# Half 0 of a two-layer block ahead of its expert stage: convolution, norm and output projection in another order, modulation sums in buffers of their own, weight slabs stored in rows of 8 KB

## What is computed

```python
mod = c_act @ w_mod + b_mod            # sh1, sc1, gt1, sh2, sc2, gt2
h = rmsnorm(x, ln_mix_g) * (1 + sc1) + sh1
q, kc, vc, ksl, vsl, kw, vw, gts, cb, cc, ch = split(h @ w_in)
o_attn = nsa_mixer(q, kc, vc, ksl, vsl, kw, vw, gts, ...)   # compressed, selected and window attention
o_conv = short_conv_mixer(ch, cb, cc, conv_w)               # cb * conv3(cc * ch)
mixed = concat(rmsnorm(o_attn, norm_attn_g), rmsnorm(o_conv, norm_conv_g))
x = x + gt1 * (mixed @ w_out)
h2 = rmsnorm(x, ln_ffn_g) * (1 + sc2) + sh2
x = x + gt2 * peer_ffn(h2, ...)
```

## Time and profile before

| | us |
|---|---|
| three runs | 1449.68, 1445.88, 1447.91 (median 1447.91) |
| profiled execution, its own time | 1451.15 |
| its span, first to last instruction | 1449.3 |

### The profile page before, as it was taken

The page is one execution under the profiler, slowest core; times in us unless marked ns, Lnnn a source line. Parts: engine busy times, 40 slices in busy tenths (PEclk is TensorE's granted clock), DMA queues, the critical chain, the costliest instruction groups (busy, mean ns, idle before and its releaser), DMA issues.

```text
span 1449.3 us, 15054 instructions
## 1 busy us (share of the span) xinstructions
PE 1160.8 (80%) x5592; PEld 674.0 (47%) x5592; DVE 745.7 (51%) x1811; ACT 487.0 (34%) x1283; POOL 370.6 (26%) x285
## 2 busy tenths in 40 slices
PE   6799885868867676666677766679988998999997
PEld 2588653422422231111122221134866887889883
DVE  5113468758769965465444445530455656652102
ACT  1022124443433433344333333321576543112201
POOL 0868202243434444433343433300000000000000
PEclk9998998999988999998998999989998999999999
DMA  9953605789999999999999999915422131114230
GB/s 365 304 218 146 246 1 201 308 326 416 412 414 420 410 412 397 421 421 407 423 386 404 396 401 422 421 65 176 174 68 107 59 117 60 60 59 160 73 116 29
DMA packets 92164, 377.58 MB, mean 261 GB/s; under 512 B 6355, under 2 KB 9596, under 8 KB 59260
## 3 DMA queue, kind: packets, MB, share of 16 engines
q0 software_dynamic: 36864, 268.45, 45.3%
q1 hardware_dynamic: 54560, 106.13, 20.4%
q10 hardware_dynamic: 668, 2.04, 0.4%
HBM read 375.54 MB, written 1.06 MB: 260 GB/s over the span
## 4 chain that ended last, share of the span: by engine, by line
PE 48%; DMA 24%; DVE 18%; ACT 7%; issue 2%; POOL 1%; SPq 1%; DVEq 0%; POOLq 0%; ACTq 0%
PE ps L87 48%; DMA AR<-in_puv,idx 20%; DVE AR L87 8%; DVE RT L87 3%; ACT L87 2%; DVE tok L87 2%; DMA mixT<-scr 1%; ACT av L87 1%; DMA W<-in_w_mod 1%; DVE acc L87 1%; DVE rowb L87 1%; DVE mixT L87 1%; ACT acc L87 1%; POOL AR L87 1%; ACT rowb L87 1%
## 5 line engine op out<-in xcount | busy, mean ns | idle before, releaser
L87 PE MATMUL ps<-AR,acc 128*64 128x512 f32 x960 | 371.2, 689 | 184.3 <-ACT acc L87 183.1
L87 POOL DMA_INDIRECT AR<-in_puv,idx x256 | 278.1, 1086 | 502.1 <-PE ps L87 394.0
L87 PE MATMUL ps<-hT,W 128*128 128x256 f32 (+2 forms) x1504 | 324.6, 374 | 2.6 <-ACT hT L87 2.5
L87 PEld LDWEIGHTS ps<-hT,W 128*128 128x128 f32 (+1 forms) x1504 | 270.4, 195 | 54.8 <-issue 15.9
L87 PEld LDWEIGHTS ps<-AR,acc 128*64 128x64 f32 x960 | 90.2, 149 | 439.3 <-ACT acc L87 356.8
L87 DVE CUSTOM_DVE_ANT_0 AR<-AR,mixT 128x1024 f32<-128x1024 f32 x128 | 156.7, 1227 | 157.0 <-DMA AR<-in_puv,idx 156.8
L87 DVE CUSTOM_DVE_ANT_0 AR<-AR,tok 128x1024 f32<-128x1024 f32 x128 | 153.1, 1219 | 66.3 <-DMA AR<-in_puv,idx 66.2
L87 ACT ACTIVATE av<-av 128x1 f32<-128x1 f32 x256 | 51.3, 200 | 311.5 <-DVE av L87 311.3
L87 ACT ACT_TABLE_LOAD x105 | 134.7, 1283 | 11.4 <-DVE tok L87 9.5
L87 PE MATMUL ps<-W,hT 128*128 128x512 f32 (+3 forms) x288 | 97.8, 497 | 0.8 <-ACT hT L87 0.8
L87 ACT ACTIVATE acc<-fold,av 128x64 f32<-128x64 f32 x240 | 83.5, 348 | 7.8
(11 more groups left out here) (230 smaller groups left out, 1087.5 us busy)
## 6 DMA issues: line engine op xcount, KB each, us to landing
W<-in_w_in SPq DMA_DIRECT2D x25, 2048.0 KB, 8.4
W<-in_w_mod SPq DMA_DIRECT2D x12, 2048.0 KB, 17.4
W<-in_w_out SPq DMA_DIRECT2D x2, 2048.0 KB, 10.3
W<-in_wq SPq DMA_DIRECT2D x2, 2048.0 KB, 10.2
AR<-in_puv,idx POOLq DMA_INDIRECT x256, 11.3
W<-in_wba SPq DMA_DIRECT2D x2, 2048.0 KB, 7.7
W<-in_wbb SPq DMA_DIRECT2D x2, 2048.0 KB, 8.6
W<-in_wo SPq DMA_DIRECT2D x2, 2048.0 KB, 7.7
```

The costliest lines, as they stand in the source:

```text
L87: ins = f(*args, **kw)
```

## The change

1. A slab is stored as 128 rows that each hold a partition's eight pieces of 512 floats one after another, and is loaded by two DMAs of 1 MB with rows of 8 KB (the slab of 280 and that of 16 columns have shorter ones in the tile).
2. The six modulation sums go to `RT`, `R_POST` and `R_LNF`, so they wait for nothing but their slab, and `flip_bias` moves behind the key and value projection. `conv_mix` and `attn_mix` no longer wait for the column sums.
3. `conv_step(0, 0)` and `conv_step(1, 0)` move between the two halves of the last convolution projection, with `weigh(3)` between them.
4. Behind the projections the attention's norm comes first, then the convolution's, then the two row sums (matmuls ahead of the mix, additions behind it); `attn_mm` waits part by part (`t_mk`). The column sums and `mod_affine` move behind `attn_mm(0, 1)`.
5. `scores(4)` no longer stands between the halves of the output projection: its matmuls stand behind `q_norm2`, its VectorE part behind `conv_mix(1)`. `weigh(4)`, `turn_p(4)`, `pv_(4)` and unit 5's scores become entries of `half1()`, which so has two entries more at its head.
6. The 29 pieces of routing ahead of the loop are gone; the loop advances 10 pieces a step for p < 3, 5 for p < 14, then 8.

```diff
         def load_w(i, after=()):
             if i < len(plan):
                 src, a, n = plan[i]
-                landed[i] = SP.dma(nc.sync.dma_start, wsem[i % NSLOT], W[:, i % NSLOT, :, 0:n],
-                                   src[:, a:a + n].rearrange("(k p) n -> p k n", p=P), after=after)
+                for k in (0, 4):
+                    landed[i] = SP.dma(nc.sync.dma_start, wsem[i % NSLOT], W[:, i % NSLOT, k:k + 4, 0:n],
+                                       src[:, 8 * a + k * n:8 * a + (k + 4) * n].rearrange("p (k n) -> p k n", k=4), after=after)
...
+        ms_buf = [RT[:, 512 * n:512 * n + 512] for n in range(3)] + [R_POST[:, 0:512], R_POST[:, 512:1024], R_LNF[:, 0:512]]
...
-        t_B = flip_bias()
...
         mod_next()
+        t_B = flip_bias()
...
                 run_step(2)
+                if (n, j2) == (2, 0):
+                    conv_step(0, 0)
+                    weigh(3)
+                    conv_step(1, 0)
...
-                       after=b.old + [t_w] + t_mix[a])
+                       after=b.old + [t_w, t_mk[a][k]])
...
-        for j in range(4):
-            conv_step(j, 0)
+        conv_step(2, 0)
+        conv_step(3, 0)
         turn_p(3)
         pv_(2)
-        b2 = ps.take()
-        for n in range(4):
-            t_mc.append(mod_cols_sum(b2, 4 * n, *t_ms[n]))
-        sh2, sc2, t_m2 = mod_affine(b2, t_mc[3], 24, V_LNF, 16)
+        pv_(3)
+        attn_root(0)
         norm_root(("c", 0), nrm[:, 0, :], cbT[:, :, 0:P], t_oc[0])
-        pv_(3)
+        rb = [mod_row_mm(*t_ms[4 + n]) for n in range(2)]
+        attn_mix(0)
         conv_mix(0)
         for n in range(2):
-            t_g1.append(mod_row_sum(2, n, *t_ms[4 + n]))
-        attn_root(0)
-        attn_mix(0)
+            t_g1.append(mod_row_add(2, n, *rb[n]))
         attn_mm(0, 0)
         for j in range(4):
             conv_step(j, 1)
         attn_add(0, 0)
-        scores(4)
         attn_mm(0, 1)
-        weigh(4)
+        b2 = ps.take()
+        for n in range(4):
+            t_mc.append(mod_cols_sum(b2, 4 * n, *t_ms[n]))
         attn_add(0, 1)
-        turn_p(4)
         norm_root(("c", 1), nrm[:, 1, :], cbT[:, :, P:2 * P], t_oc[1])
-        q_norm(0, [])
+        q_norm1(0)
+        sh2, sc2, t_m2 = mod_affine(b2, t_mc[3], 24, V_LNF, 16)
+        q_norm2(0, [])
+        scores_mm(4)
         q_project(0, 0)
         conv_mix(1)
...
+        scores_add(4)
         routes = [route(0, [])]
...
-        pv_(4)
         while (0, 0) not in t_idx or (0, 0) not in t_gw:
             advance(routes[0], 1)
-        scores_mm(5)
-        advance(routes[0], 29)
-        scores_add(5)
...
-            yield [lambda: weigh(5), lambda: scores_mm(6)]
+            yield [lambda: weigh(4), lambda: scores_mm(5)]
+            yield [lambda: scores_add(5), lambda: turn_p(4)]
+            yield [lambda: weigh(5), lambda: pv_(4), lambda: scores_mm(6)]
...
-            advance(routes[0], 4 if p < 12 else 8)
+            advance(routes[0], 10 if p < 3 else 5 if p < 14 else 8)
...
+    def slabs(w, cuts=None):
+        cuts = cuts or range(0, w.shape[1] + 1, 512)
+        return np.concatenate([w[:, lo:hi].reshape(8, P, hi - lo).transpose(1, 0, 2).reshape(P, -1)
+                               for lo, hi in itertools.pairwise(cuts)], axis=1)
```

More of the change, by code:

```diff
@@ L1 @@
+import itertools
 import math
@@ L235, in build @@
         R_LNF, R_POST, R_G1, R_G2 = (rowb[:, r, :] for r in range(4))
+        RT = sb("RT", [P, 6 * 256])
         t_neg = V(nc.vector.memset, tok2[32:33, 1, 0:8], NEG)
@@ L306, in mod_cols_sum, with mod_row_mm, mod_row_add @@
             return t2
-        def mod_row_sum(r, n, buf, t):
+        def mod_row_mm(buf, t):
             b = ps.take()
-            t = PE(mm, b.t[:, :], ones, buf, start=True, stop=True, after=b.old + [t, t_in])
+            return b, PE(mm, b.t[:, :], ones, buf, start=True, stop=True, after=b.old + [t, t_in])
+        def mod_row_add(r, n, b, t):
             o = rowb[:, r, n * 512:n * 512 + 512]
@@ L660, in build, with conv_step @@
                   lambda: (cmp_turn(0, 0), cmp_turn(0, 1)),
-                  lambda: (cmp_add(0, 0), cmp_add(0, 1), pv_(0), pv_(1), turn_p(2), scores(3), weigh(3)),
+                  lambda: (cmp_add(0, 0), cmp_add(0, 1), pv_(0), pv_(1), turn_p(2), scores(3)),
                   ]
+        def conv_step(j, a):
+            c0, c = a * P, slice(a * P, a * P + P)
+            wc = [PV[:, V_CW + r * 4 + j:V_CW + r * 4 + j + 1] for r in range(3)]
+            o = oc[:, j, c]
+            t = V(ts_, o, z[:, j, c0:c0 + P], wc[0], None, MUL, after=[t_cv[2, j // 2], t_zz])
+            t = V(stt, o, z[:, j, c0 + 1:c0 + 1 + P], wc[1], o, MUL, ADD, after=[t])
+            t = V(stt, o, z[:, j, c0 + 2:c0 + 2 + P], wc[2], o, MUL, ADD, after=[t])
+            t = V(tt_, o, o, cbT[:, j, c], MUL, after=[t, t_cv[0, j // 2]])
+            t_oc[a].append(V(tt_, cbT[:, j, c], o, o, MUL, after=[t]))
         oc = ccT
+        t_oc = [[], []]
         t_zz = G(nc.gpsimd.memset, z[:, :, 0:2], 0.0)
@@ L685, in build @@
                 run_step(2)
+                if (n, j2) == (2, 0):
+                    conv_step(0, 0)
+                    weigh(3)
+                    conv_step(1, 0)
         run_step(99)
-        t_oc = []
-        def conv_step(j, a):
-            c0, c = a * P, slice(a * P, a * P + P)
-            wc = [PV[:, V_CW + r * 4 + j:V_CW + r * 4 + j + 1] for r in range(3)]
-            o = oc[:, j, c]
-            t = V(ts_, o, z[:, j, c0:c0 + P], wc[0], None, MUL, after=[t_cv[2, j // 2], t_zz])
-            t = V(stt, o, z[:, j, c0 + 1:c0 + 1 + P], wc[1], o, MUL, ADD, after=[t])
-            t = V(stt, o, z[:, j, c0 + 2:c0 + 2 + P], wc[2], o, MUL, ADD, after=[t])
-            t = V(tt_, o, o, cbT[:, j, c], MUL, after=[t, t_cv[0, j // 2]])
-            t_oc[a].append(V(tt_, cbT[:, j, c], o, o, MUL, after=[t]))
         t_cn = {}
@@ L713, in conv_mix @@
             for j in range(4):
-                t_mix[a].append(V(stt, mixT[:, 4 + j, c], oc[:, j, c], PV[:, V_NC + j:V_NC + j + 1], n, MUL, MUL,
-                                  after=[e, t_oc[a][j]] + t_mc))
+                t_mk[a][4 + j] = V(stt, mixT[:, 4 + j, c], oc[:, j, c], PV[:, V_NC + j:V_NC + j + 1], n, MUL, MUL,
+                                   after=[e, t_oc[a][j], t_B])
+                t_mix[a].append(t_mk[a][4 + j])
         osqs = (osq0, osq0)
@@ L722, in attn_root @@
             t = A(act, osqs[a], O[a].t[:, :].rearrange("p (j t) -> p j t", j=4), ACT.Square,
-                  after=[stage[3 + 4 * a, "O"], stage[1 + 4 * a, "O"]] + t_g1 + t_c["o", 0] + t_c["o", 1] + t_jx[-1:]
+                  after=[stage[3 + 4 * a, "O"], stage[1 + 4 * a, "O"]] + t_c["o", 0] + t_c["o", 1] + t_jx[-1:]
                   + ([t_n[0]] if a else []))
@@ L731, in attn_mix @@
                 t = V(stt, mixT[:, j, a * P:a * P + P], O[a].t[:, j * P:j * P + P], PV[:, V_NA + j:V_NA + j + 1],
-                      rats[a], MUL, MUL, after=[e, t_os[a]] + t_mc + free)
+                      rats[a], MUL, MUL, after=[e, t_os[a], t_B] + free)
+                t_mk[a][j] = t
                 t_mix[a].append(t)
             O[a].free = [t]
-        t_oc, t_mix = [[], []], [[], []]
+        t_mix, t_mk = [[], []], [{}, {}]
         t_mc, t_g1 = [], []
```

18 lines of the change are left out of this document (7 added, 11 removed).

## The result

| | kernel before | changed kernel |
|---|---|---|
| median of 20 runs, us | 1447.83 | 1436.81 |
| lowest, highest | 1441.00, 1453.39 | 1430.94, 1451.51 |
| profiled execution, its own time | 1451.15 | 1435.28 |
| its span | 1449.3 | 1433.5 |

The ratio is 0.9934 (95% interval 0.9915 to 0.9953): faster by 0.66%, 11.0 us between the medians, where 19.7 were forecast. The measured median, 1436.8, lies above the forecast's range (1423 to 1434).

The account below looks back on a forecast made before the run. Bound: TensorE's chain up to the first gather, then full DMA engines, with the second layer moving as a block. Terms -9.4 + 4.9 - 11.5 - 1.2 - 2.5 = -19.7 gave 1428.2 us on the median, range 1423 to 1434.

Parts of the forecast that it names:

- flips: Bias flips moved behind the key and value projection: no table wait or low clock, convolution projections 6.8 + 2.6 sooner, -9.4 us.
- 8 KB rows at the start: Initial loads: queues alternate packet by packet, so longer slab rows delay `x` and `K`; q projection 4.9 us later.
- last projection to queries, clock included: From the last convolution projection to the queries: reordering gives -10.0 and the clock -1.5, together -11.5 us.
- first gather: Sum of the terms ahead of the gathers: first gather moves by -16.0 us, from 225.55 to about 209.5.
- ramp, from the first gather to p = 20: Start of the gathers: earlier first dots, their gain almost all spent on moved work; forecast up to p = 16, -1.2 us.
- 8 KB rows beside the gathers: Six slabs loading while DMA engines are full take 5.0 us each instead of 5.4; -2.5 us, bounds 0 and -2.5.
- `x` is not on time: Rival at the start: `x` and `K` not delayed, so -0.8 instead of +4.9, 1422.5 us; chance 0.20.
- long rows are not slow to read: Rival at the start: long rows at wide steps read slowly, costing 44 us at 150 GB/s, 1467 us; chance 0.04.
- the halves of a slab do not pay one after another: Rival at slab loads: both half-slab DMAs pay their fixed part of about 2 us in series, 1431.3 us; chance 0.08.
- The clock ... I take -1.5.: Output projection: TensorE busy ahead of it, so full clock, 7.1 instead of 8.8 us; -1.5, bounds 0 and -4.3.
- From there I take today's pace.: Ramp after `half1` starts at G + 19.6 (G the first gather): 13 steps in 91.1 us, p = 16 at G + 122.9.
- The rival that has the ramp give it back: Ramp: two more entries cost 4 us and longer first three steps 6 us, 1438.2 us; chance 0.13.

Follow-up runs that it names:

- e1: The changed kernel run again with no edit, for a second profile and the scatter; median 1436.9 us, ratio 0.9936.
- e4: The kernel before with only the slabs in rows of 8 KB, two DMAs a slab; median 1446.8 us, ratio 1.0009.
- The extra matmuls: Six unread 512-column matmuls among the column and norm sums behind the output projection; alone on the changed kernel, median 1436.1 us, ratio 0.9909.
- e14: The changed kernel with four more VectorE instructions ahead of the sum finishing sc1, so it comes after GpSimd's multiply has begun; median 1443.6 us, ratio 0.9982.
- e7: The changed kernel with the kernel before's order between the first gather and p = 14, two entries fewer; median 1436.1 us, ratio 0.9928.
- e11: The changed kernel with `x`, `K`, then the slabs on one queue, and six extra 512-column matmuls behind the output projection; median 1429.4 us, ratio 0.9885.
- e15: The changed kernel with GpSimd's first modulation multiplies waiting for VectorE's small sc1 instructions, and six extra 512-column matmuls; median 1433.7 us, ratio 0.9892.
- e16: The changed kernel with `x`, `K`, slabs on one queue, the old ramp order, late projections in parts and six extra matmuls; median 1420.3 us, ratio 0.9801.
- e8: The changed kernel with only the six slabs that load beside the gathers in rows of 2 KB; median 1437.1 us, ratio 0.9919.
- e5: The changed kernel with six unread 512-column matmuls among the column and norm sums behind the output projection; median 1436.1 us, ratio 0.9909.
- e10: The changed kernel with each of four second-layer projections among the last gathers cut into four parts of two matmuls; median 1430.6 us, ratio 0.9899.
- e3: The changed kernel with `x` first, then the four slabs, then `K` on SP's queue; median 1441.0 us, ratio 0.9966.

## Why the prediction was too low

| term | forecast | measured |
|---|---|---|
| flips | -9.4 | convolution projections 5.1 sooner with the q projection 4.7 later: -9.8 |
| 8 KB rows at the start | +4.9 | +4.7 (43.40 against 38.66) |
| last projection to queries, clock included | -11.5 | -8.5 and, in e1, -11.3 |
| first gather | -16.0 | -13.6; -16.4 in e1 |
| ramp, from the first gather to p = 20 | -1.2 | +1.3; +3.9 in e1 |
| lead at p = 20 | -17.2 | -12.3; -12.5 in e1 |
| 8 KB rows beside the gathers | -2.5 | 0 (-2.6 on the kernel before, e4) |
| lead at p = 84 | -19.7 | -12.3; -12.6 in e1 |
| median | -19.7 | -11.0 |

The mechanisms of the front were right: wait and low clock of the flips, the 1 : 1 alternation and its size, the split into two DMAs at no cost, the output projection 7 us behind the last projection. That also decides three rivals: `x` is not on time, long rows are not slow to read, and the halves of a slab do not pay one after another (the fourth slab landed at 28.0, before at 29.8, and VectorE finds it at 35.19 without a wait). The Trainium skill, page "DMA: Bandwidth & Descriptors", section "Anatomy of one DMA", gives the fixed part of about 2 us for a DMA on GpSimd's path, and the slabs are on SP's; in this trace no such part of one slab DMA adds to the next.

That the first gather came near its time (209.2 in e1, 209.5 forecast) is in part luck: the output projection was 1.9 us better than laid out, and the way from its end to the queries took 13.6 us (11.6 in e1) instead of 9.9.

Three steps failed.

**"The clock ... I take -1.5."** The projection did get its full clock: 13.90 for its two halves, where 8.80 and 7.13 stood. But the forecast moved 4 us of one-column matmuls without reckoning with a low clock behind them. Before, one stood there at 0.58, from 169.4 to 175.3, though a wait of 2.26 us lies there too; now it falls on the scores and the queries, and in part on the first combinations of the ramp. The low clock at the output projection was another one, behind waits, and that is the one that went. The extra matmuls show the size, some 3 us at p = 20, with e14 as an exception that stays open. The forecast's bounds had 0 as the worse end here, since the row was read as the cost of a wait alone, and no term had a clock that gets lower.

**"From there I take today's pace."** The ramp was timed by its dots. These came as said, with 1.85 MB less fetched, so the term of -1.2 was the wrong way round: +1.3, and +3.9 in e1. The rival that has the ramp give it back is the nearest of all to the median (1438.2), and p = 3 came at 246.0 where 241.3 had been laid out. But the cause that it named, two more entries, is not what e7 shows: without them p = 20 is at 360.6 against 360.5. Even with the clock kept, p = 20 is 149 us behind the first gather in the new order (e11 148.9, e15 149.5) and 149.9 in the old (e16), not 146. That the early dots are worth nothing over the old order is e7's result. What costs these 3 us stays open: all these kernels have the probabilities and values of unit 4 behind the first routing, where before they stood ahead of it, and none of them was moved back.

**"Rows of 8 KB beside the gathers: -2.5."** Nothing, by e8. The rate came (422 against 377 GB/s with full engines), but the term took a shorter transfer for a shorter time, and the engines stood idle for what was saved. (Six times the difference of the two rates, 0.39 us, is also 2.3 and not 2.5.)

These make up 7.4 of the 8.7 by p = 84, the first two terms having been 0.6 better than forecast; this goes by one profile of before, which itself lay 3.3 above its median. The other 1.3 lies between p = 84 and the median, where single executions differ by 4 us, and where now and then 9 us of the hold come on top; it is not resolved. The bound on the start (+7.7) did not have the hold: being late there was priced as lateness, and not as losing a race that stood 1.2 us away.

## What to carry to other kernels

Ahead of a stretch that the DMA engines fill, count progress in bytes and not in steps: a step that comes sooner with less in flight pays the difference back. Moving a batch of one-column matmuls moved the low clock behind them as well; look at what stands there in the new order. Six wide matmuls among them kept the clock here. And when a change makes one engine's chain later, list what the others start at that time: a 0.17 us instruction cost 6 because it came a microsecond late, and a 7 us projection that TensorE had time for starved the gathers until it was cut into four.

## What the runs showed of the hardware

- This VectorE instruction, with two inputs in SBUF, does not get through while a GpSimd multiply over SBUF runs: 6.32, 6.87, 6.26 and 5.83 us for a 128 x 8 instruction (e5, e14, e4, e10; 0.17 alone), and 1.50 in e3, where it came late in the multiply; each ends with GpSimd's 7.01 us. The Trainium skill, page "SBUF — State Buffer", section "SBUF: two separate sides", says that the two share a port pair as an exclusive lock, held for a whole instruction by whichever starts first. The rows agree where GpSimd started first; that VectorE holds GpSimd off, no run here shows. VectorE's copies out of PSUM (1.90 us for four) took no longer beside GpSimd's next instruction.
- The granted clock fell while TensorE was busy all the time: it ran one-column matmuls from 179.5 to 184.3 in the changed kernel, and the clock was 0.50 from 181.8 to 184.3, 0.61 from 179.5 to 189.6 and 0.55 from there to 199.8. With 512-column matmuls after every eight of them it stayed at 1.00 (179.9 to 190.6 in e15).
- Two queues alternate packet by packet with 8 KB against 4 KB as with 2 KB against 4 KB: 80 to 80, 62% to 40% of the time.
- Plain loads in rows of 8 KB moved more with full engines than those in rows of 2 KB: from 539 to 558, with gathers beside them, 422 GB/s (changed kernel) against 377 (e8).
